# Entering the last feed-forward by token halves, and other lengths for the side work

## The chip, the cores and the metric

The kernel runs on one NeuronCore of a Trainium2 chip. The metric is the device time of one execution in microseconds (us). The engines are TensorE (PE, with its weight loads PEld), VectorE (DVE), ScalarE (ACT) and GpSimd (POOL); SyncE (SP) issues the weight DMAs. All of them run in order and wait for each other through semaphores.

## The reference

Two transformer blocks follow each other on 256 tokens of width 1024, in fp32. The first mixes softmax attention ("fox"), a gated delta rule and stick-breaking attention, then does a cross-attention to a memory and a feed-forward with a convolution. The second is this one:

```python
h = rmsnorm_2(x, ffn1_pre_g[l])
f = swiglu(h, ffn1_w_gate[l], ffn1_w_up[l], ffn1_w_down[l])
x = x + MACARON_WEIGHT * rmsnorm_2(f, ffn1_post_g[l])
h = rmsnorm_2(x, mix_pre_g[l])
proj = h @ w_in[l]
...
attn = moba_attention(to_heads(q), to_heads(k), to_heads(v), slopes)
pool = multiscale_pool(p_in, pool_w[l], pool_scale[l])
y = jnp.concatenate([attn, pool], axis=-1) @ w_out[l]
x = x + rmsnorm_2(y, mix_post_g[l])
h = rmsnorm_2(x, xa_pre_g[l])
mem_n = rmsnorm_2(mem, mem_g[l])
c = memory_cross_attention_2(h, mem_n, xa_wq[l], xa_wkv[l], xa_wo[l])
x = x + rmsnorm_2(c, xa_post_g[l])
h = rmsnorm_2(x, ffn2_pre_g[l])
f = swiglu(h, ffn2_w_gate[l], ffn2_w_up[l], ffn2_w_down[l])
x = x + MACARON_WEIGHT * rmsnorm_2(f, ffn2_post_g[l])
```

`swiglu` is `(silu(h @ w_gate) * (h @ w_up)) @ w_down` with an inner width of 2816. With 256 tokens the MoBA attention is causal attention over one block.

## The kernel before

**Chunks.** All weight matrices are cut into 178 chunks of 1 MB (`build_chunks`). SP loads chunk c into one of three buffers `raw`, once VectorE has freed it. ScalarE rounds it to fp32r (`hi`, line 1443, `whi`), VectorE takes the rest (`lo`, line 1693, `wlo`), and TensorE multiplies three products (high by high, high by low, low by high) in place of one fp32 product. `hi` and `lo` of chunk c+2 are queued when chunk c is multiplied (`LEAD`). A chunk has two halves, `("mm", c, 0)` and `("mm", c, 1)`. Kinds of chunk: W (256 output features by all 256 tokens; for each of 8 slices k of the inner axis four matmuls, of 512 and of 256 columns, lines 1139 and 1142), V and R (tokens by features, 24 matmuls of 512 columns, lines 1158 and 1170), A and O. A group of R chunks ("rows") adds up `w_out_2`, `xa_wo_2` or a down projection in four PSUM banks, two for each half of the tokens (128).

**Seams.** At the end of such a group comes the norm. For each token half: `post1` (ACT, square with sum, line 1668), `post_r` (1671, 1672), `post0` (DVE, by the gain, 1937), `post2` (DVE, into the residual `x_tok`, 1942); then for the next layer's norm `ns` (ACT, square with sum, 1461), `nr` (1465, 1466) and `nd` (DVE, times 1/rms, 1703). TensorE then transposes (`nt`, line 1184) 128x128 pieces by five groups of slices, ScalarE writes the high part of the transposed, scaled slice (`nh`, 1472), VectorE the low part (`nl`, 1708), and the next chunk's matmuls wait for `nl` of their slice. In the seam into the last feed-forward (chunks 143, 144 are the last two of `xa_wo_2`, chunk 145 is the first gate chunk) each R chunk is multiplied for both token halves, except the last one, which does token half 0 first and then token half 1.

**Side work and its planner.** Attention heads and the delta rule are chains of small steps ("links": `sc` scores, `sm` row maximum, `ex` exp, `pn` normalize, `pt` transpose, `pc` copy, `pv` values, `oc` and `ol` high and low part of the output). `build_plan` writes the order of all engines at build time. It keeps a rough clock for every engine, advanced by the costs in `ROUGH`. Between halves and quarters of chunks (`mma` is the first quarter of a half) `hook` asks `fits` for each chain whether the inputs of its next link are ready by the clock of TensorE plus a tolerance `EARLY`, and if so places that link there. Nothing is reordered on the chip, so a link put too early makes its engine wait with everything behind it. Heads of one attention run in two lanes with banks 4, 5 and 6, 7.

**Banks.** PSUM has 8 banks. `take` notes who read a bank last, and the next user waits for that step (`bank_wait`). An R chunk waits at its start for the readers of both token halves' banks.

## Time and profile before

| | us |
|---|---|
| median of 3 runs | 1211.7 |
| lowest and highest | 1209.04, 1212.9 |
| profiled execution, its own time | 1205.77 |
| its span, first to last instruction | 1204.0 |

| engine | busy us | share of the span |
|---|---|---|
| PE | 1156.5 | 96% |
| PEld | 1005.7 | 84% |
| DVE | 811.0 | 67% |
| ACT | 614.9 | 51% |
| POOL | 80.9 | 7% |

The span runs from the first to the last instruction of the core; the execution's own time has a little more around it. Busy TensorE is counted from modelled ends of matmuls, so that the gaps between its instructions are what can be read best. In a timeline each row is one or several merged instructions with start, duration, engine, line, what is written from what, and in brackets how long the engine had been idle and what released it. In a table of windows PEclk is the granted TensorE clock, 1.00 for 2.4 GHz and 0.50 for 1.2 GHz.

### The profile page before, as it was taken

Reading aid. Unit: us, or ns where it says so; the run is one execution under the profiler, and the core shown is the slowest. Engines: PE = TensorE matmul, PEld = TensorE weight load, DVE = VectorE, ACT = ScalarE, POOL = GpSimd, SP = SyncE. Lnnn points to the kernel's source line nnn. Section 1 sums busy time; section 2 is a strip of 40 time slices with the busy share of each in tenths; the row PEclk is TensorE's granted clock in tenths of the full one; section 3 lists DMA queues with packets and bytes.
Section 4 is the critical chain, followed back from the end, with each engine's and each line's share of the span. In section 5 each row is a group of like instructions: output and inputs, shape, how many; then the busy total and the mean of one; then the engine's idle time right before and its main releaser. Section 6 shows DMA issues by size and latency. Waiting matters only on the chain.

```text
span 1204.0 us, 16670 instructions
## 1 busy us (share of the span) xinstructions
PE 1156.5 (96%) x6747; PEld 1005.7 (84%) x6747; DVE 811.0 (67%) x865; ACT 614.9 (51%) x780; POOL 80.9 (7%) x114
## 2 busy tenths in 40 slices
PE   6999999999998899999999999999999997999997
PEld 6878988888987789999888888888776886888886
DVE  6877565855778667787647777647666656777743
ACT  6556344434767556555436444436345546444442
POOL 8001100200000000000000000002700000000000
PEclk9999999999999999999999999999999998999999
DMA  8644332433565336555665656555443524666550
GB/s 255 189 143 138 105 106 82 130 105 105 210 210 173 108 104 202 191 188 176 210 197 166 197 177 202 182 201 182 167 140 105 178 85 142 191 192 192 181 203 36
DMA packets 144132, 193.95 MB, mean 161 GB/s; under 512 B 6136, under 2 KB 121208, under 8 KB 144056
## 3 DMA queue, kind: packets, MB, share of 16 engines
q1 hardware_dynamic: 142856, 188.43, 48.1%
q0 software_dynamic: 1200, 4.46, 1.0%
q8 instruction: 54, 0.88, 0.3%
q14 instruction: 22, 0.18, 0.0%
HBM read 191.82 MB, written 1.05 MB: 160 GB/s over the span
## 4 chain that ended last, share of the span: by engine, by line
PE 85%; DVE 7%; ACT 4%; issue 2%; DMA 1%; SPq 0%; ACTq 0%; DVEq 0%
PE banks L1139 23%; PE banks L1170 19%; PE banks L1131 13%; PE banks L1142 11%; PE banks L1158 5%; DVE wlo L1693 2%; PE banks L1149 2%; ACT whi L1443 2%; PE banks L1383 1%; PE banks L1184 1%; PE banks L1214 1%; PE banks L1303 1%; PE banks L1257 1%; PE banks L1266 1%; DMA raw<-in_w_in 1%
## 5 line engine op out<-in xcount | busy, mean ns | idle before, releaser
L1693 DVE TENSOR_TENSOR wlo<-raw,whi 128x2048 fp32r<-128x2048 f32 x178 | 407.4, 2292 | 187.7 <-ACT whi L1443 187.6
L1443 ACT ACTIVATE whi<-raw 128x2048 fp32r<-128x2048 f32 x178 | 339.4, 1910 | 182.2 <-PE banks L1170 88.5
L1139 PE MATMUL banks<-xhl,whi 128*128 128x512 f32 x1248 | 403.9, 405 | 3.4 <-DVE fq_ L1968 1.6
L1142 PEld LDWEIGHTS banks<-xhl,wlo 128*128 128x128 f32 x1248 | 235.7, 189 | 55.8
L1142 PE MATMUL banks<-xhl,wlo 128*128 128x256 f32 x1248 | 246.9, 279 | 0.0
L1139 PEld LDWEIGHTS banks<-xhl,whi 128*128 128x128 f32 x1248 | 192.6, 190 | 11.8 <-issue 6.9
L1131 PE MATMUL banks<-xhl,whi 128*128 128x256 f32 x912 | 165.0, 284 | 0.0
L1131 PEld LDWEIGHTS banks<-xhl,whi 128*128 128x128 f32 x912 | 142.1, 192 | 0.5 <-DVE xhl L1708 0.2
L1131 PE MATMUL banks<-xhl,wlo 128*128 128x256 f32 x456 | 129.0, 283 | 0.0
L1170 PE MATMUL banks<-whi,hh 128*128 128x512 f32 x264 | 102.7, 389 | 0.0
L1170 PE MATMUL banks<-wlo,hh 128*128 128x512 f32 x264 | 102.7, 389 | 0.0
L1170 PE MATMUL banks<-whi,hl 128*128 128x512 f32 x264 | 102.7, 389 | 0.0
L1131 PEld LDWEIGHTS banks<-xhl,wlo 128*128 128x128 f32 x456 | 87.5, 192 | 0.0
L1662 ACT ACTIVATE hh<-SG 128x512 fp32r<-128x512 f32 x33 | 20.9, 632 | 93.0 <-DVE SG L1984 93.0
L1170 PEld LDWEIGHTS banks<-whi,hl 128*128 128x128 f32 x264 | 49.6, 188 | 10.4
L1170 PEld LDWEIGHTS banks<-whi,hh 128*128 128x128 f32 x264 | 49.6, 188 | 10.1
L1170 PEld LDWEIGHTS banks<-wlo,hh 128*128 128x128 f32 x264 | 49.6, 188 | 10.1
L1980 DVE TENSOR_REDUCE CA<-banks 128x512 f32<-128x1024 f32 x22 | 27.0, 1225 | 25.9 <-PE banks L1142 25.9
L1950 DVE SCALAR_TENSOR_TENSOR CA<-banks,pcol,CA 128x255 f32<-128x255 f32 (+1 forms) x88 | 36.4, 476 | 8.4 <-ACT CA L1644 8.0
L1988 DVE TENSOR_TENSOR hl<-SG,hh 128x512 fp32r<-128x512 f32 x33 | 22.9, 693 | 27.3 <-ACT hh L1662 27.3
L1158 PE MATMUL banks<-whi,xhl 128*128 128x512 f32 x96 | 35.1, 422 | 0.0
L1708 DVE SCALAR_TENSOR_TENSOR xhl<-banks,pcol,xhl 128x256 fp32r<-128x256 f32 x56 | 24.2, 479 | 8.8 <-ACT xhl L1472 8.7
(354 smaller groups left out, 1505.5 us busy)
## 6 DMA issues: line engine op xcount, KB each, us to landing
raw<-in_w_in SPq DMA_DIRECT2D x40, 1024.0 KB, 5.3
raw<-in_w_up SPq DMA_DIRECT2D x22, 1024.0 KB, 5.1
...
```

The lines of the kernel that those rows point to most:

```text
L1131: ins = pe.matmul(o, a[:, k, cols_], v[:, k, :], start=(k == 0 and i == 0), stop=(k == KD - 1 and i == 2))
L1139: pe.matmul(bank(b[m]), wh[:, k, m * P:(m + 1) * P], both[:, k, :, :].rearrange("p a t -> p (a t)"), start=(k == 0), stop=(k == KD - 1), s ...
L1142: ins = pe.matmul(bank(b[m])[:, 0:T], wl[:, k, m * P:(m + 1) * P], Xh[:, k, :], start=False, stop=(k == KD - 1), skip_group_check=True)
L1149: ins = pe.matmul(bank(b[part])[:, m * T:(m + 1) * T], a[:, k, o:o + P], v[:, k, :], start=(k == 0 and i == 0), stop=(k == NH - 1 and i == 2))
L1158: ins = pe.matmul(bank(b[t]), v[:, k, t * P:(t + 1) * P], a[:, kk, :], start=(k == 0 and i == 0), stop=(k == KD - 1 and i == 2))
L1170: ins = pe.matmul(bank(b[2 * t + nb]), v[:, k, t * P:(t + 1) * P], a[:, kk, nb * 512:(nb + 1) * 512], start=(ch["first"] and kk == 0 and i ...
L1443: act.activation(whi[c % RING][:, :], raw[c % RING][:, :], ACT.Copy).then_inc(act_done, 1)
L1693: dve.tensor_tensor(wlo[c % RING][:, :], raw[c % RING][:, :], whi[c % RING][:, :], ALU.subtract).then_inc(dve_done, 1)
L1708: dve.scalar_tensor_tensor(l_[:, k, :], turned(name, k), pcolumn(name, k), h_[:, k, :], ALU.mult, ALU.subtract).then_inc(dve_done, 1)
L1950: ins = dve.scalar_tensor_tensor(d, bank(chunks[c]["banks"][0])[:, m * T:(m + 1) * T - s], pcolumn("ffn_conv", (2 - s) * 2 * KF + a * KF + ...
L1980: dve.tensor_reduce(mat(CA[i % 2][:, 1, :]), halves(c), AX_X, ALU.add).then_inc(dve_done, 1)
L1988: dve.tensor_tensor(hl[:, 2 * i:2 * i + 2, :], mat(SG[i % 2]), hh[:, 2 * i:2 * i + 2, :], ALU.subtract).then_inc(dve_done, 1)
```

## The change

It has three parts.

1. **The seam into the last feed-forward** (`seam` in place of two `mm` and a `norm_turn`). Chunks 143 and 144 are multiplied for token half 0 first, then both for token half 1. The norm of half 0 is queued while half 1 is still multiplied. Transposes (`nt2`), high parts (`nh2`) and low parts (`nl2`) are done for each token half by itself, 128 wide and not 256, 8 and 8. The first gate chunk is multiplied by token halves too: for each slice two matmuls of 2x128 columns and two of 128, once for each half. The banks of the last feed-forward's chunks are exchanged (gate and up start in 0 to 3, the down projection adds up in 4 to 7), and `hi` and `lo` of chunk 146 come later.
2. **The pooled products one chunk sooner.** The pooling's matmuls (`pl_mm`) are placed in chunk 129 and no more in chunk 130, and in banks 0 and 1, not 2 and 3. `w_out_2` takes its banks in the order (2, 3, 0, 1), and an R chunk waits for the banks of a token half only when it comes to that half.
3. **Other lengths for the planner.** `ROUGH` has costs for each kind of attention, chunk costs go by kind, `hi` cannot end before the DMA of its chunk (5.8 us after the `lo` that frees the buffer), a link that begins on DVE or ACT is compared with that engine's clock, `EARLY` goes from 0.2 to 0.5, the turn of `mem_g_2` may not come before `add` of the chunk before, and the MoBA heads of a lane are two short chains joined.

VectorE at the seam into the last feed-forward, before (L1693 is `lo`, L1937 and L1942 `post0` and `post2`, L1703 `nd`, L1708 `nl`, L1975 the first gate chunk's reduction):

```order
L1693 TENSOR_TENSOR wlo<-raw,whi 128x2048 x3
L1937 SCALAR_TENSOR_TENSOR xs<-banks,gain 128x1024
L1942 SCALAR_TENSOR_TENSOR x_tok<-xs,small,x_tok 128x1024
L1937 SCALAR_TENSOR_TENSOR xs<-banks,gain 128x1024
L1942 SCALAR_TENSOR_TENSOR x_tok<-xs,small,x_tok 128x1024
L1703 TENSOR_SCALAR xs<-x_tok,small 128x1024 x2
L1708 SCALAR_TENSOR_TENSOR xhl<-banks,pcol,xhl 128x256 x8
L1693 TENSOR_TENSOR wlo<-raw,whi 128x2048
L1975 TENSOR_REDUCE CA<-banks 128x512
```

and after (L1793 `lo`, L2044 and L2049 `post0` and `post2`, L1803 `nd`, L1814 `nl2`):

```order
L1793 TENSOR_TENSOR wlo<-raw,whi 128x2048 x2
L2044 SCALAR_TENSOR_TENSOR xs<-banks,gain 128x1024
L2049 SCALAR_TENSOR_TENSOR x_tok<-xs,small,x_tok 128x1024
L1803 TENSOR_SCALAR xs<-x_tok,small 128x1024
L2044 SCALAR_TENSOR_TENSOR xs<-banks,gain 128x1024
L1814 SCALAR_TENSOR_TENSOR xhl<-banks,pcol,xhl 128x128 x3
L2049 SCALAR_TENSOR_TENSOR x_tok<-xs,small,x_tok 128x1024
L1814 SCALAR_TENSOR_TENSOR xhl<-banks,pcol,xhl 128x128 x5
L1803 TENSOR_SCALAR xs<-x_tok,small 128x1024
L1793 TENSOR_TENSOR wlo<-raw,whi 128x2048
L1814 SCALAR_TENSOR_TENSOR xhl<-banks,pcol,xhl 128x128 x8
L1793 TENSOR_TENSOR wlo<-raw,whi 128x2048
```

The `lo` of chunk 146 moved from ahead of `post0` to between `nd` of token half 1 and the eight `nl2` of that half.

VectorE at the first MoBA heads, before (L1863 and L1865 are `pn`, L1849 to L1857 `sm`, L1693 `lo` of chunk 130):

```order
L1863 RECIPROCAL small<-small 128x2
L1865 TENSOR_SCALAR S<-S,small 128x128
L1865 TENSOR_SCALAR S<-S,small 128x256
L1863 RECIPROCAL small<-small 128x2
L1865 TENSOR_SCALAR S<-S,small 128x128
L1865 TENSOR_SCALAR S<-S,small 128x256
L1849 SCALAR_TENSOR_TENSOR S<-cmask,banks 128x384
L1852 TENSOR_REDUCE small<-S 128x1 x2
L1857 TENSOR_SCALAR small<-small 128x2
L1693 TENSOR_TENSOR wlo<-raw,whi 128x2048
```

and after (L1970 and L1972 are `pn`, L1956 to L1964 `sm`, L1793 the `lo`):

```order
L1970 RECIPROCAL small<-small 128x2
L1972 TENSOR_SCALAR S<-S,small 128x128
L1972 TENSOR_SCALAR S<-S,small 128x256
L1970 RECIPROCAL small<-small 128x2
L1972 TENSOR_SCALAR S<-S,small 128x128
L1972 TENSOR_SCALAR S<-S,small 128x256
L1793 TENSOR_TENSOR wlo<-raw,whi 128x2048
L1956 SCALAR_TENSOR_TENSOR S<-cmask,banks 128x384
L1959 TENSOR_REDUCE small<-S 128x1 x2
L1964 TENSOR_SCALAR small<-small 128x2
```

The `lo` now stands before the `sm` of head 2. On TensorE the first quarter of chunk 128 stands ahead of the transposes of head 0 (chunk 128 came after them).

TensorE in the memory branch, before (L1158 is chunk 47, `mv`; L1184 the transposes of `mem_g_2`; L1214 the sum `hn_sum` of `mq0`):

```order
L1158 MATMUL banks<-whi,mhl 128x512 x2
L1158 MATMUL banks<-wlo,mhl 128x512
L1158 MATMUL banks<-whi,mhl 128x512
L1184 MATMUL banks<-ident,xs 128x128 x16
L1158 MATMUL banks<-whi,mhl 128x512
L1158 MATMUL banks<-wlo,mhl 128x512
L1158 MATMUL banks<-whi,mhl 128x512 x2
L1158 MATMUL banks<-wlo,mhl 128x512
L1158 MATMUL banks<-whi,mhl 128x512
L1214 MATMUL banks<-S,ones 128x512
```

and after (L1233 is chunk 47, L1307 the sum, L1262 the transposes):

```order
L1233 MATMUL banks<-whi,mhl 128x512 x2
L1233 MATMUL banks<-wlo,mhl 128x512
L1233 MATMUL banks<-whi,mhl 128x512 x2
L1233 MATMUL banks<-wlo,mhl 128x512
L1233 MATMUL banks<-whi,mhl 128x512 x2
L1233 MATMUL banks<-wlo,mhl 128x512
L1233 MATMUL banks<-whi,mhl 128x512
L1307 MATMUL banks<-S,ones 128x512
L1262 MATMUL banks<-ident,xs 128x128 x16
L1233 MATMUL banks<-whi,mhl 128x512
```

The transposes moved behind the whole of chunk 47 and behind the sum.

The core of the diff:

```diff
-EARLY, EARLY_LONG = 0.2, 0.8
+EARLY, EARLY_LONG = 0.5, 0.6
...
-         "sc": 1.3, "sm": 1.4, "ex": 0.85, "pn": 0.8, "pt": 0.7, "pc": 0.5, "pv": 0.7, "oc": 0.4, "ol": 0.45,
...
+         ("sc", "moba"): 0.65, ("sm", "moba"): 1.5, ("ex", "moba"): 0.95, ("pn", "moba"): 0.85, ("pt", "moba"): 0.67,
...
-            behind = self.ended["mm", args[0] - RING, 1]
+            behind = max(self.ended["mm", args[0] - RING, 1], self.ended["lo", args[0] - RING] + 5.8)
...
-                b = 4 * ((left + f - 1) % 2)
+                b = 4 * (left % 2)
...
-    rows("w_out_2", 4, "y5", "post", 0, (2, 3, 0, 1))
+    rows("w_out_2", 4, "y5", "post", (2, 3, 0, 1), (2, 3, 0, 1))
...
-    ffn(2, "ffn2_w_gate_2", "ffn2_w_up_2", "ffn2_w_down_2", 0, "post", 0)
+    for ch in out[-2:]:
+        ch["by_token"] = True
+    first = len(out)
+    ffn(2, "ffn2_w_gate_2", "ffn2_w_up_2", "ffn2_w_down_2", 0, "post", 4)
+    out[first]["by_token"] = True
...
+        first_ = "pe" if callable(link_[0]) else link_[0][0]
+        if first_ != "pe":
+            return ready_ <= max(pl.clock["pe"], pl.clock[first_]) + EARLY
...
+    def seam(c, name, base):
+
+        last_, gate_ = c + 1, c + 2
...
+        split(c + LEAD)
+        pl.add("pe", "mm", c, 0)
+        pl.add("pe", "mm", last_, 0)
+        pl.add("act", "post1", last_, 0)
+        pl.add("dve", "post0", last_, 0)
+        pl.add("act", "post_r", last_, 0)
+        pl.add("dve", "post2", last_, 0)
+        pl.add("pe", "mm", c, 1)
+        pl.add("act", "hi", last_ + LEAD)
+        norm_scale(name, 0)
+        pl.add("pe", "mm", last_, 1)
...
+        pl.bank_wait["nt", name, 4] = [("nl2", name, 0, turns(name)[0][-1])]
...
+        pl.add("act", "post1", last_, 1)
+        pl.add("dve", "post0", last_, 1)
+        for j in groups:
+            pl.add("pe", "nt2", name, 0, j)
+        halves_of(0, 0, 1)
+        pl.add("act", "post_r", last_, 1)
+        pl.add("dve", "post2", last_, 1)
+        halves_of(0, 2, 3, 4)
+        norm_scale(name, 1)
+        pl.add("dve", "lo", last_ + LEAD)
...
+        pl.add("pe", "mm", gate_, 0)
+        for j in groups:
+            pl.add("pe", "nt2", name, 1, j)
+        halves_of(1, *groups)
+        split(gate_ + LEAD)
+        pl.add("pe", "mm", gate_, 1)
...
-    finished[id(turn_m2)] = pl.ended["nd", "mem_g_2", 1]
+    finished[id(turn_m2)] = max(pl.ended["nd", "mem_g_2", 1], pl.ended["add", c - 1])
...
-        side.append(heads_of("moba", [lane, lane + 2, lane + 4, lane + 6]))
...
+        side.append(heads_of("moba", [lane, lane + 2]) + heads_of("moba", [lane + 4, lane + 6]))
...
-    pl.take(("pl_mm",), (2, 3), ("pl_l",))
-    mm(c, mid=[("pe", "pl_mm"), ("act", "pl_h"), ("dve", "pl_l")])
...
+    pl.take(("pl_mm",), (0, 1), ("pl_l",))
+    mm(c + 2, mid=[("pe", "pl_mm"), ("act", "pl_h"), ("dve", "pl_l")])
...
-                for t in () if 0 not in quarters else (part, 1) if ch["kind"] == "R" and part == 0 else (part,):
+                for t in () if ch["kind"] == "R" or 0 not in quarters else (part,):
...
+                elif ch["kind"] == "W" and ch["by_token"]:
+                    both, s = BOTH[ch["x"]], slice(part * P, (part + 1) * P)
+                    for k in range(KD):
+                        pe.wait_ge(dve_done, at(*plan.fresh[c], part, k))
+                        for m in range(2):
+                            pe.matmul(bank(b[m]).rearrange("p (a t) -> p a t", a=2)[:, :, s], wh[:, k, m * P:(m + 1) * P],
+                                      both[:, k, :, s], start=(k == 0), stop=(k == KD - 1), skip_group_check=True)
+                        for m in range(2):
+                            ins = pe.matmul(bank(b[m])[:, s], wl[:, k, m * P:(m + 1) * P], Xh[:, k, s], start=False,
+                                            stop=(k == KD - 1), skip_group_check=True)
...
+                        for step in plan.bank_wait.get(("mm", c, half), []) if part == 0 else []:
+                            pe.wait_ge(DONE[plan.engine[step[0]]], at(*step))
```

## Rows read from the trace of the kernel before

**Rows 1.** The page: busy us and share; line engine | busy, mean ns.

```profile
...
PE 1156.5 (96%) x6747; PEld 1005.7 (84%) x6747; DVE 811.0 (67%) x865; ACT 614.9 (51%) x780; POOL 80.9 (7%) x114
...
L1443 ACT ACTIVATE whi<-raw 128x2048 fp32r<-128x2048 f32 x178 | 339.4, 1910 | 182.2 <-PE banks L1170 88.5
```

**Rows 2.** Waits of TensorE: releaser, us, times, longest us.

```profile
...
PE banks L1184 <- DVE xs L1703: 7.0, 2, 6.8
...
PE banks L1184 <- DVE mq_ L1968: 2.7, 1, 2.7
...
PE banks L1170 <- DVE qk_ L1968: 2.2, 1, 2.2
```

**Rows 3.** Timeline of TensorE, memory branch.

```profile
...
385.13 2.72 PE L1184 MATMUL banks<-ident,xs 128*128 128x128 f32 x16 [2.71 <-DVE mq_ L1968]
```

**Rows 4.** Windows: busy PE, PEld, DVE, ACT, POOL; granted clock, DMA.

```profile
...
386.00:390.00 4.00, 4.00 (x17) 3.54 (x16) 4.00 (x9) 3.20 (x8) 0.00 (x0) 0.57 0.67 235
867.00:871.00 4.00, 4.00 (x14) 2.81 (x13) 1.34 (x4) 2.17 (x5) 0.00 (x0) 0.57 0.00 0
1007.00:1014.00 7.00, 2.73 (x13) 2.73 (x14) 3.73 (x6) 4.12 (x12) 0.64 (x2) 0.52 0.35 127
1014.00:1015.00 1.00, 1.00 (x8) 0.91 (x7) 1.00 (x3) 0.97 (x3) 0.00 (x0) 0.91 0.00 0
```

**Rows 5.** Timeline of TensorE at the first MoBA heads.

```profile
...
862.66 0.39 PE L1158 MATMUL banks<-wlo,xhl 128*128 128x512 f32 x1
862.89 0.39 PE L1158 MATMUL banks<-whi,xhl 128*128 128x512 f32 x1
865.85 0.55 PE L1361 MATMUL banks<-ident,S 128*128 128x128 f32 x3 [2.57 <-DVE S L1865]
```

**Rows 6.** Waits of TensorE in the MoBA stretch.

```profile
...
PE banks L1170 <- DVE y5l L1878: 1.2, 1, 1.2
PE banks L1361 <- DVE y5l L1878: 1.1, 2, 0.7
```

**Rows 7.** Timeline of TensorE, end of the cross-attention.

```profile
...
974.21 0.95 PE L1363 MATMUL banks<-ident,S 128*128 128x128 f32 x7 [1.63 <-DVE y5l L1878]
```

**Rows 8.** Timeline of the seam into the last feed-forward.

```profile
...
1001.10 2.29 DVE L1693 TENSOR_TENSOR wlo<-raw,whi 128x2048 fp32r<-128x2048 f32 x1 [3.15 <-ACT whi L1443]
...
1001.86 1.03 ACT L1668 ACTIVATE xs<-banks 128x1024 f32<-128x1024 f32 x1 [0.79 <-PE banks L1170]
...
1003.42 1.22 DVE L1937 SCALAR_TENSOR_TENSOR xs<-banks,gain 128x1024 f32<-128x1024 f32 x1
...
1004.10 0.39 PE L1170 MATMUL banks<-whi,y5l 128*128 128x512 f32 x1
...
1004.68 1.28 DVE L1942 SCALAR_TENSOR_TENSOR x_tok<-xs,small,x_tok 128x1024 f32<-128x1024 f32 x1
...
1008.64 1.06 ACT L1461 ACTIVATE xs<-x_tok 128x1024 f32<-128x1024 f32 x1 [0.65 <-DVE x_tok L1942]
...
1010.46 0.75 DVE L1703 TENSOR_SCALAR xs<-x_tok,small 128x1024 f32<-128x1024 f32 x1 [1.12 <-ACT small L1466]
...
1011.27 3.36 PE L1184 MATMUL banks<-ident,xs 128*128 128x128 f32 x16 [6.78 <-DVE xs L1703]
...
1013.77 3.01 DVE L1708 SCALAR_TENSOR_TENSOR xhl<-banks,pcol,xhl 128x256 fp32r<-128x256 f32 x7 [0.73 <-ACT xhl L1472]
...
1020.34 1.22 DVE L1975 TENSOR_REDUCE CA<-banks 128x512 f32<-128x1024 f32 x1 [0.22 <-PE banks L1142]
```

**Rows 9.** Groups of VectorE, 92 to 290 us.

```profile
...
L1834 DVE SCALAR_TENSOR_TENSOR gS<-gS,gX,banks 128x128 f32<-128x128 f32 x16 | 4.5, 344 | 7.5 <-PE banks L1305 7.5
```

**Rows 10.** Groups of ScalarE, 92 to 290 us.

```profile
...
L1547 ACT ACTIVATE gKt<-banks,gcols 128x128 f32<-128x128 f32 x8 | 3.1, 386 | 0.0
```

**Rows 11.** Timeline of TensorE: transposes in a stream.

```profile
...
938.96 1.69 PE L1184 MATMUL banks<-ident,xs 128*128 128x128 f32 x14
```

**Rows 12.** Waits of TensorE, fox and delta rule.

```profile
...
PE banks L1257 <- DVE gY L1813: 0.7, 3, 0.4
```

81 lines of the change are left out of this document (61 added, 20 removed), and 7 rows, old and new, of the table ROUGH.

## Prediction, made before the changed kernel ran

> **What bounds the kernel now.** I read the page first: TensorE is busy for 1156.5 us of a span of 1204.0 [rows 1]. So only what TensorE waits for, what it does at half clock, and what it does more or less of can move the time. The second view is the table of TensorE's waits. It shows one long wait, 6.8 us at the seam into the last feed-forward (`nd`, line 1703), and then 2.7, 2.6 and 2.2 us at three places in the side work [rows 2, 5]. The third is the granted clock in windows: it lay at 1.2 GHz (0.50) for a while behind three of these waits. Over 386 to 390 us its mean was 0.57, over 867 to 871 also 0.57, and over 1007 to 1014 it was 0.52 [rows 4]. In the first two stretches TensorE was busy throughout, so they cost 4.0 x (1 - 0.57) = 1.7 us each. In the third it mostly waited. The last view is the timeline of each place.
>
> **The seam, in the times of the trace before.** `post1` of token half 0 starts at 1001.86, the last matmul ends at 1004.10 + 0.39 = 1004.5, the last `nd` starts at 1010.46, the transposes at 1011.27, and the gate chunk's reduction at 1020.34 [rows 8]. Doing half 0 of chunk 144 one half earlier lets `post1` start 2.7 us earlier (half a chunk; 1004.5 less 1001.86), at 999.1. From there:
> - `post1` takes 1.1 with its accumulator read, `post0` 1.22, `post2` 1.28 [rows 8]. The `lo` that held `post0` before (1001.10 to 1003.39) is gone from there. `post2` of half 0 ends at 1002.9.
> - ScalarE has `hi` of chunk 146 queued ahead of `ns`. It waits for chunk 143 to end (1001.8) and takes 1.9 us (line 1443 [rows 1]), so `ns` starts at 1003.8. From `ns` to `nd` takes 1.8 us (1008.64 to 1010.46) and `nd` 0.75 [rows 8]: first transpose at 1006.4. The long wait shrinks from 6.8 to 1.9 us.
> - ScalarE does `post1` of half 1 from 1005.5 to 1006.65, then `nh2`. VectorE does `post0` until 1007.9, three `nl2`, `post2` until 1010.3, and the other five `nl2`. An operation of that shape (scalar_tensor_tensor, 128x128 out of PSUM) cost 4.5 / 16 = 0.28 us in a stream [rows 9], and 128x128 on ScalarE 0.39 [rows 10]. The last `nl2` of half 0 ends at 1011.8, and the token-0 half of the gate chunk with it, at 1012.3. In between TensorE waits in pieces.
> - `ns`, `nr`, `nd` of half 1 start when `post2` ends: `nd` ends at 1012.9. Now VectorE has the 2.29 us `lo` of chunk 146 [rows 8] in front of the eight `nl2` of half 1. They start at 1015.2 and end at 1017.7. Nothing needs this `lo` before the next chunk, but the `nl2` are queued behind it and TensorE behind them. TensorE has the eight transposes and can begin the token-1 half at 1015.7.
> - The token-1 half is 8 slices of four matmuls. Fourteen 128-column transposes, each with its own weights, took 1.69 us, 0.11 each after taking off the end of the last [rows 11]. I take 0.11 for the 128-column and 0.12 for the 256-column ones: 0.45 a slice, 3.6 us, end at 1019.4. Bound below: columns alone, half of the (1020.2 - 1014.6) = 5.6 us of the chunk before, 2.8 us. Bound above: all at 1.2 GHz, at least twice 2.8.
>
> Before, the chunk ended at about 1020. So the seam as a whole gives 0.5 us, although its wait falls by 4.9: the rest is given back as 1.7 us more TensorE work (7.2 for 5.6) and as new waits for `nl2`. Bounds: +2.0 (columns alone, and the `nh2` without delay) and -2.0 (the clock stays low into the token-1 half). The 8 + 8 operations on ScalarE and VectorE in place of 8 have no other user waiting there. `lo` of 147 comes at 1018 to 1020.5 and is wanted at 1025. The DMA freed by `lo` of 146 lands long before its use.
>
> The Trainium skill, TensorE: Matmul & The Clock Gate, section "LDWEIGHTS", says a weight load takes its number of columns over 1.2 GHz, whatever streams. That speaks against this part: 64 loads of 128 columns for the gate chunk would be an estimated 6.8 us, not 3.4. Its section "Back-to-back issue gap" has about 81 ns for a pair at 128 columns, by which a half would be an estimated 2.6 us. By the first the seam gives the 0.5 us, by the second an estimated 1.5. The transposes at 0.11 [rows 11] agree with the first.
>
> **The memory branch.** The transposes of `mem_g_2` waited 2.71 us for an `add` on `mq_`, after only a quarter of chunk 47 had been issued [rows 3]. Now the remaining 18 matmuls of that chunk (about 4.1 us) and a sum stand in front of them. They need nothing late, and the `add` has then ended. The wait goes, and with it the cause of the slow stretch of [rows 4]: 2.7 + 1.7 = 4.4 us. Bounds: 2.7 if the clock falls anyway, 5.0 with small gaps behind it.
>
> **The MoBA stretch.** The transposes of head 0 waited 2.57 us for `pn` [rows 5]. Now the first quarter of chunk 128 is ahead of them: six matmuls at 0.23 (862.66 to 862.89 [rows 5]), 1.4 us. The wait is 1.2, and I expect the clock to stay up: 1.4 + 1.7 [rows 4]. `lo` of chunk 130 is now ahead of `sm` of head 2 and delays that head by 2.3 us, but its transposes come two chunks later. The wait of 2.2 us for `add` on `qk_` [rows 2] was `w_out_2` asking for banks 0 and 1, which chunk 130 had just written. Now half 0 goes to banks 2 and 3, read long ago, and a score step and half 1 come later: 2.2 gone. The pooled products come at about 876 in their new place and I cost them at nothing: their windows on GpSimd are done before that, and the banks' reader is the copy of chunk 128, which ends then; were it late, they would wait as they did before, some tenths. Of the waits for `y5l`, the last, 1.2 us before chunk 134, stays. The two of 1.1 together become one of about 0.7 (its longest [rows 6]), since copy, values and output of head 7 follow one another with nothing beside them: 0.4. Sum 5.7 us. Bounds: 3.5 (clock still low, another 0.5 in waits) and 7.
>
> **The cross-attention's end.** `pv` of head 0 is now ahead of the last half of chunk 140, so `y5l` comes earlier. Its wait of 1.63 us [rows 7] becomes 0.3, and `sc` of head 3 gets a wait of 0.3 for the `add` now behind `pn` and `ol`: 1.0 (0.5 to 1.5).
>
> **Fox and delta rule.** Some 36 pieces on TensorE stand elsewhere. The wait that recurs there before is 0.7 us in 3 [rows 12], so nothing is to be won, and the tolerance of 0.5 allows small new waits. I cost it at 0.5 us; bounds +0.5 and -1.5.
>
> **Sum.** 0.5 + 4.4 + 5.7 + 1.0 - 0.5 = 11.1 us less. The profiled execution took 1205.77 (span 1204.0 and 1.8 around it), so a like one would take 1194.7. The median of the runs shown is 1211.7, 5.9 above the profiled one, and the forecast for a median is 1200.6.
>
> **Rivals.**
> - *The clock does not come back.* The low stretches follow the new waits (1.2 us at head 0, the pieces at the seam). For: the clock fell behind waits of 2.6 and 2.7 us, so little is missing. Against: a wait of 1.2 is less than half of either. Then 3.4 us less is won: 1204.
> - *The seam is dearer.* TensorE runs in short pieces from 1006 to 1015, the clock stays at 1.2 GHz as in 1007 to 1014 [rows 4], and the token-1 half takes 7.2 in place of 3.6: 1204.2. Against: the clock was back at 0.91 in 1014 to 1015 [rows 4] after 3 us of transposes only.
> - *The seam is cheaper.* Narrow matmuls go by their columns and waits fall further: 1.5 to 2 us more, 1198.8.
> - *The change does not do what it says in the side work.* VectorE's queue only moves the MoBA waits: only the 2.2 there, the memory branch, and nothing else, 6.1 us: 1205.6.
> - *Slower.* Links put early by the larger tolerance make TensorE wait at piece after piece in fox and delta rule, where it is busy without pause. It decides from 11.6 / 36 = 0.32 us a piece. The longest there before is 0.4 [rows 12]. At 0.4 each it is 14.4 us, the total 1211.7 - 11.6 + 14.4 = 1214.5. Against: VectorE has room there and the new costs are closer to the trace.
>
> **How the numbers follow.** Forecast 0.50 (its own range 1198 to 1203), clock 0.19, seam dearer 0.08, seam cheaper 0.10, side work 0.08, slower 0.05. About 0.3% (3.6 us) is what a measurement can tell from no change here, since the three runs before lie 3.9 us apart. The bounds add up to savings between 3.2 and 16; two medians scatter by 2 us. I leave out a tenth at each end: 1195 to 1207. Faster (under 1208.1) 0.88: all cases but the last, less 0.07 for two of them together. Within 0.3% 0.07, slower 0.05.
>
> **What would show it.** No wait before the transposes of `mem_g_2`, clock 1.00 over that place and over the first MoBA heads, a wait of about 1.2 us at head 0, none before chunk 131. At the seam: first transposes 1.9 us after the last row matmul, `nl2` of half 1 in one stream right behind a `lo`, and 14.9 us (before 15.5) from the last row matmul to the end of the gate chunk. A saving at the seam of several us, or a `nl2` stream that starts with `nd`, would make that step wrong. Waits of 0.3 us and more by the dozen between 90 and 290 us would make the whole wrong.

## The result and the profile after

| | before | after |
|---|---|---|
| median of 5 runs, side by side | 1209.38 us (1205.07 to 1212.9) | 1196.2 us (1195.82 to 1200.65) |
| profiled execution, and its span | 1205.77, 1204.0 us | 1200.3, 1198.6 us |
| mean granted clock in it | 0.991 | 0.992 |

The ratio is 0.9903, 95% interval [0.9876, 0.9931]: 11.7 us less, between 8 and 15. It is close to the ratio of the means, 1197.8 to 1209.6. The forecast was 1200.6 in 1195 to 1207. The profiled execution after is one of the two slower ones of its five, and the one before (1205.77) is near the fastest, so the two traces differ by only 5.4 us of span. They are therefore compared stretch by stretch. The length of a stretch is taken between two matmuls that both kernels have.

| stretch | before | after | difference | forecast |
|---|---|---|---|---|
| start to the 400th matmul | 69.5 | 71.6 | +2.1 | 0 |
| to the first matmul on the memory tokens (fox, delta rule) | 284.8 | 285.9 | +1.0 | +0.5 |
| to the first matmul on the memory branch's output | 67.2 | 63.5 | -3.6 | -4.4 |
| to the first down-projection | 148.3 | 149.9 | +1.6 | 0 |
| to the cross-attention's first value chunk (MoBA) | 358.3 | 352.4 | -6.0 | -5.7 |
| to the last row matmul | 76.0 | 75.0 | -1.0 | -1.0 |
| to the end (the seam) | 199.5 | 199.9 | +0.3 | -0.5 |

The page's line on the engines (busy us; share of the span; instructions) against [rows 1]:

```profile
PE 1161.4 (97%) x6779; PEld 1011.5 (84%) x6779; DVE 811.4 (68%) x873; ACT 616.5 (51%) x788; POOL 82.2 (7%) x114
```

There are 32 matmuls more (the gate chunk by halves) and eight operations more on each of VectorE and ScalarE, as the diff says. TensorE is busy for 4.9 us longer in a span that is 5.4 us shorter: its idle time fell from 47.5 to 37.2 us.

TensorE's waits (releaser; us, times, longest us) against [rows 2, 6, 12]:

```profile
PE banks L1277 <- DVE xs L1803: 2.0, 1, 2.0
...
PE banks L1277 <- DVE xhl L1814: 1.3, 2, 1.0
PE banks L1350 <- DVE gY L1920: 1.3, 5, 0.5
PE banks L1454 <- DVE S L1972: 1.2, 1, 1.2
PE banks L1248 <- DVE y5l L1985: 1.2, 1, 1.2
...
PE banks L1430 <- DVE mq_ L1880: 0.8, 1, 0.8
...
PE banks L1307 <- DVE mq_ L1880: 0.5, 1, 0.5
...
PE banks L1456 <- DVE y5l L1985: 0.2, 1, 0.2
```

The 6.8 at the seam is 2.0 and 1.3. The 2.7 on `mq_` and the 2.2 on `qk_` are gone, with 0.8 and 0.5 new in the memory branch. The 2.6 at MoBA's head 0 is 1.2. The 1.63 at the end of the cross-attention is 0.2. `gY` in the delta rule takes 1.3 in five where it took 0.7 in three.

Windows of the changed kernel (us; busy PE, PEld, DVE, ACT, POOL; granted clock; DMA share, GB/s), against [rows 4]:

```profile
390.00:394.00 4.00, 4.00 (x27) 3.37 (x26) 2.46 (x6) 2.85 (x7) 0.00 (x0) 1.00 0.76 231
...
422.00:426.00 4.00, 4.00 (x14) 3.21 (x13) 2.29 (x1) 1.11 (x3) 0.00 (x0) 0.57 0.08 20
...
866.00:870.00 4.00, 2.97 (x15) 2.17 (x16) 3.01 (x7) 3.23 (x6) 1.48 (x2) 1.00 0.11 44
...
1002.00:1009.00 7.00, 6.42 (x30) 6.45 (x31) 6.33 (x12) 3.83 (x12) 0.64 (x2) 0.52 0.23 76
1009.00:1010.00 1.00, 1.00 (x10) 1.00 (x10) 0.15 (x1) 0.21 (x1) 0.00 (x0) 0.92 0.00 0
```

The clock is up behind `mem_g_2` and at the MoBA heads, where it was 0.57 before. At 422 us there is a stretch at 1.2 GHz that the trace before did not have: that is the +1.6 of the table. At the seam TensorE is now at 1.2 GHz while it works (6.42 of 7 us busy). Before, it was at 1.2 GHz mostly while it waited (2.73 of 7).

The timeline of the seam (start, us, engine, line, operation, [idle before]), against [rows 8]:

```profile
998.28 0.39 PE L1248 MATMUL banks<-whi,y5l 128*128 128x512 f32 x1
1000.62 0.98 PE L1277 MATMUL banks<-ident,xs 128*128 128x128 f32 x7 [1.95 <-DVE xs L1803]
1002.58 0.45 PE L1277 MATMUL banks<-ident,xs 128*128 128x128 f32 x1 [0.97 <-DVE xhl L1814]
1002.71 0.76 PE L1203 MATMUL banks<-xhl,whi 128*128 128x256 f32 x2
...
1003.59 0.73 PE L1203 MATMUL banks<-xhl,whi 128*128 128x256 f32 x2
...
1009.39 0.96 PE L1277 MATMUL banks<-ident,xs 128*128 128x128 f32 x7
...
1012.23 0.45 PE L1203 MATMUL banks<-xhl,whi 128*128 128x256 f32 x2
...
1012.69 0.45 PE L1203 MATMUL banks<-xhl,whi 128*128 128x256 f32 x2
...
1014.53 0.67 PE L1214 MATMUL banks<-xhl,whi 128*128 128x512 f32 x2
```

The first wait is 1.95 us. The token-0 half runs without a pause, at 0.85 us a slice (1002.71 to 1003.59 and on), since the clock is low. Only behind it come the transposes of half 1 (1009.39). The token-1 half takes 0.46 a slice (1012.23 to 1012.69) and ends at 1014.5, 15.86 us after the last row matmul. Before, it was 15.57.

On VectorE in the same place:

```profile
1006.20 0.75 DVE L1803 TENSOR_SCALAR xs<-x_tok,small 128x1024 f32<-128x1024 f32 x1 [0.63 <-ACT small L1559]
1006.86 2.28 DVE L1793 TENSOR_TENSOR wlo<-raw,whi 128x2048 fp32r<-128x2048 f32 x1
1010.19 0.35 DVE L1814 SCALAR_TENSOR_TENSOR xhl<-banks,pcol,xhl 128x128 fp32r<-128x128 f32 x1 [1.04 <-ACT xhl L1572]
1010.85 2.18 DVE L1814 SCALAR_TENSOR_TENSOR xhl<-banks,pcol,xhl 128x128 fp32r<-128x128 f32 x7 [0.31 <-ACT xhl L1572]
```

The `lo` does stand between `nd` and the `nl2` of half 1. But VectorE waits 1.04 us behind it for ScalarE, which waits for the transposes: in this execution the `lo` holds nothing up.

The first MoBA heads, against [rows 5]:

```profile
867.03 0.55 PE L1454 MATMUL banks<-ident,S 128*128 128x128 f32 x3 [1.20 <-DVE S L1972]
```

The end of the cross-attention, against [rows 7]: the wait for `y5l` at head 0 and the new one for `qk_` at the scores of head 3.

```profile
968.01 1.06 PE L1456 MATMUL banks<-ident,S 128*128 128x128 f32 x8 [0.24 <-DVE y5l L1985]
969.27 1.96 PE L1436 MATMUL banks<-xk_,qk_ 128*128 128x256 f32 x8 [0.20 <-DVE qk_ L2075]
```

### The profile page after: what moved, and what is told of

Read it like the earlier page. It is cut to its first block, busy times and chain, and to the rows that moved or that the text cites. A ratio compares the mean times of both kernels' runs of the same rounds, so it can differ in the third digit from the quotient of the medians.

```text
span 1198.6 us, 16754 instructions
## 1 busy us (share of the span) xinstructions
PE 1161.4 (97%) x6779; PEld 1011.5 (84%) x6779; DVE 811.4 (68%) x873; ACT 616.5 (51%) x788; POOL 82.2 (7%) x114
## 4 chain that ended last, share of the span: by engine, by line
PE 87%; DVE 6%; ACT 4%; issue 2%; DMA 1%; SPq 0%; ACTq 0%; DVEq 0%
PE banks L1214 24%; PE banks L1248 20%; PE banks L1196 14%; PE banks L1217 12%; PE banks L1233 4%; PE banks L1224 2%; DVE wlo L1793 2%; ACT whi L1536 2%; PE banks L1476 1%; PE banks L1307 1%; PE banks L1350 1%; PE banks L1396 1%; PE banks L1359 1%; DMA raw<-in_w_in 1%; PE banks L1436 1%
## 5 line engine op out<-in xcount | busy, mean ns | idle before, releaser
L1793 DVE TENSOR_TENSOR wlo<-raw,whi 128x2048 fp32r<-128x2048 f32 x178 | 407.4, 2293 | 180.8 <-ACT whi L1536 180.7
L1214 PE MATMUL banks<-xhl,whi 128*128 128x512 f32 x1232 | 399.1, 405 | 3.4 <-DVE fq_ L2075 1.6
L1214 PEld LDWEIGHTS banks<-xhl,whi 128*128 128x128 f32 x1232 | 190.1, 190 | 12.0 <-issue 6.8
L1233 PE MATMUL banks<-whi,xhl 128*128 128x512 f32 x96 | 34.9, 418 | 0.0
L1102 POOL TENSOR_TENSOR gMs<-gM,lev 128x512 f32<-128x512 f32 x12 | 21.3, 1776 | 139.0 <-DVE gM L1901 96.6
```

The costliest lines, as they stand in the source:

```text
L1102: pool.tensor_tensor(gMs[l % 2][:, :, :], gM[:, :, :], lev[:, l, :].unsqueeze(1).to_broadcast([P, NH, P]), ALU.mult).then_inc(pool_done, 1)
L1214: pe.matmul(bank(b[m]), wh[:, k, m * P:(m + 1) * P], both[:, k, :, :].rearrange("p a t -> p (a t)"), start=(k == 0), stop=(k == KD - 1), s ...
L1233: ins = pe.matmul(bank(b[t]), v[:, k, t * P:(t + 1) * P], a[:, kk, :], start=(k == 0 and i == 0), stop=(k == KD - 1 and i == 2))
L1793: dve.tensor_tensor(wlo[c % RING][:, :], raw[c % RING][:, :], whi[c % RING][:, :], ALU.subtract).then_inc(dve_done, 1)
```

## Experiments

All of them are read by the stretches of the same table. Where a run took one execution only, its total says little and its trace is what counts. Short stretches at 1.2 GHz (low stretches below) come at different places in different executions; each costs 1.7 us where TensorE is busy (3.4 us long: 4 us at a mean of 0.57 in [rows 4]). So the places are given with each time.

### The seam taken back, and the seam alone

`no_seam` is the changed kernel with the seam of before:

```diff
...
-    seam(c + 2, "ffn2_pre_g_2", 4)
-    pl.add("pool", "gain_load", 3)
-    c += 5
-    for _ in range(KF + KF // 2 - 1):
+    mm(c + 2)
+    mm(c + 3)
+    c += 4
+    pl.add("pool", "gain_load", 3)
+    norm_turn("ffn2_pre_g_2", 0)
+    for _ in range(KF + KF // 2):
...
```

> The changed kernel with the old seam into the last feed-forward (whole chunks, whole turns, old banks there); parts 2 and 3 stay. Theory 1 (the seam gives nothing, since what it wins in waiting it pays in narrow matmuls and low clock): 11 to 12 us under before, within 1 us of the changed kernel; from the last row matmul to the end of the gate chunk 15.5 us as before, against 15.9 in the changed kernel. Theory 2 (the seam is where the gain is): only 5 to 8 us under before.

Measured: 1198.76 us (1194.75 to 1200.18, 6 runs), 0.9892 [0.987, 0.9914] of before. The changed kernel has 0.9903 [0.9876, 0.9931]. That is 13 us less than its own runs of before, where the first theory said 11 to 12: the gain is there without the seam.

`seam_only` is the kernel before with part 1 alone: costs, tolerances, banks, pooled products and MoBA chains stay as in before (the lines are against the changed kernel).

```diff
...
-EARLY, EARLY_LONG = 0.5, 0.6
+EARLY, EARLY_LONG = 0.2, 0.8
...
-    rows("w_out_2", 4, "y5", "post", (2, 3, 0, 1), (2, 3, 0, 1))
+    rows("w_out_2", 4, "y5", "post", 0, (2, 3, 0, 1))
...
```

> The kernel before with part 1 alone (seam by token halves and the exchanged banks of the last feed-forward). Theory 1: within 1 us of before, TensorE's wait before the first transposes down from 6.8 to about 1.9 us, the gate chunk's end 15 to 16 us behind the last row matmul as before. Theory 2: 3 to 5 us faster than before.

Measured: 1209.11 us (1205.74 to 1213.12, 12 runs), 0.9989 [0.9975, 1.0004] of before: 1.3 us less, between 3.0 less and 0.5 more. In its trace the gate chunk ends 15.73 us after the last row matmul, and in that of `no_seam` 15.49. What follows from both: the seam is worth between nothing and 3 us of the 11.7.

### The gate chunk whole

`gate_whole` keeps the rows and the norm by halves, but takes the gate chunk in one piece behind both (`halves_of(1, ...)` first, then `mm(gate_, 0)` and `mm(gate_, 1)`).

```diff
-    out[first]["by_token"] = True
...
-        pl.add("pe", "mm", gate_, 0)
         for j in groups:
             pl.add("pe", "nt2", name, 1, j)
...
+        pl.add("pe", "mm", gate_, 0)
         pl.add("pe", "mm", gate_, 1)
```

> The changed kernel, but the first gate chunk is multiplied whole (512 and 256 columns) after both token halves are turned. If the narrow matmuls are the price (7 us of TensorE for 5.6), the stretch from the last row matmul to the end of the gate chunk gets shorter than 15.9 us, about 15. If the token-0 half is in the shadow of the waits for nd of half 1 anyway, it gets longer: nl2 of half 1 starts 10.5 us behind the last row matmul, the first slice follows, and 5.6 us of gate chunk end at 16.5 us or later.

Measured: 1198.69 us in one run; the gate chunk ends 19.1 us after the last row matmul, and from there to the end of the kernel it is 203.1 us, against 15.9 and 199.9. It gets longer, as the second branch of the expectation said, and by more than its 16.5. TensorE (timeline of this kernel):

```profile
1002.17 1.76 PE L1276 MATMUL banks<-ident,xs 128*128 128x128 f32 x7 [3.98 <-DVE xs L1802]
...
1004.85 1.19 PE L1213 MATMUL banks<-xhl,whi 128*128 128x512 f32 x2
...
1006.27 1.05 PE L1213 MATMUL banks<-xhl,whi 128*128 128x512 f32 x2
```

Without the token-0 half TensorE waits 3.98 us for the `nd` of half 1, and the clock stays low for 13.7 us. Halving the chunk therefore buys 3.2 us (one trace of each, and one seam differs by up to 1.4 between traces, see below), and the halved rows and norm without it are worse than the seam of before. The seam stands or falls by the gate chunk.

### The clock held up in the seam

`warm_seam` is the changed kernel with eight idle matmuls of 512 columns in the 1.95 us wait; `warm_lo_late` has them too, and `lo` of chunk 146 behind the `nl2` of half 1.

```diff
+        pl.add("pe", "warm")
         for j in groups:
             pl.add("pe", "nt2", name, 0, j)
...
+            def warm():
+                ...
+                for i in range(8):
+                    ins = pe.matmul(bank(7), y5h[:, i % 4, 0:P], ..., start=True, stop=True)
```
```diff
-        pl.add("dve", "lo", last_ + LEAD)
...
         halves_of(1, *groups)
+        pl.add("dve", "lo", last_ + LEAD)
```

> The changed kernel with eight extra matmuls of 512 columns (1.8 us, their result is overwritten) on TensorE between the last row matmul and the first transposes, where it waits 1.95 us. Theory 1 (the low clock from 3.7 to 10.5 us behind the last row matmul is what holds the token-0 half until 10.7 us): the clock stays at 2.4 GHz or falls later, the token-0 half ends with nl2 at about 7.5 us, and the gate chunk ends at 14.5 us in place of 15.9; the nl2 of half 1 still wait for lo of chunk 146. Theory 2 (the clock follows the pieces of work behind, not this wait): the clock falls at the same place and the stretch stays at 15.9 us.

> The changed kernel with eight idle 512-column matmuls in the wait after the last row matmul, and with the lo of chunk 146 put behind the nl2 of token half 1 on VectorE. Theory (two causes add up: the low clock costs the seam about 0.9 us, and the lo in front of the nl2 of half 1 costs whatever part of its 2.3 us lies on the path when the clock is up): the gate chunk ends 13 to 13.5 us after the last row matmul, 198 us or less from there to the end. Rival (the lo is hidden in this form too, because the token-0 half of the gate chunk is what ends last there): 15.0 and 199.0 again, as with the idle matmuls alone.

`warm_seam` measured 1199.06 us in one run; the gate chunk ended 15.0 us after the last row matmul and the kernel 199.0 us after it: 0.9 us less than the changed kernel. A low stretch came all the same, later and half as long, and the token-0 half ended at 9.8 us where the theory had 7.5:

```profile
1000.00:1004.00 4.00, 2.82 (x21) 2.35 (x20) 3.58 (x7) 3.60 (x12) 0.00 (x0) 1.00 0.00 2
1004.00:1008.00 4.00, 3.78 (x19) 3.79 (x20) 3.36 (x7) 1.65 (x4) 0.64 (x2) 0.57 0.35 131
1008.00:1010.00 2.00, 1.66 (x16) 1.45 (x14) 1.54 (x4) 1.40 (x5) 0.00 (x0) 1.00 0.07 12
```

`warm_lo_late` measured 1196.86 us in one run, 199.8 from the last row matmul to the end. The first `nl2` of half 1 starts 10.64 us after the last row matmul in both (1008.94 in `warm_seam` and 1005.95 here):

```profile
1002.84 0.75 DVE L1812 TENSOR_SCALAR xs<-x_tok,small 128x1024 f32<-128x1024 f32 x1 [0.63 <-ACT small L1568]
1005.95 0.35 DVE L1823 SCALAR_TENSOR_TENSOR xhl<-banks,pcol,xhl 128x128 fp32r<-128x128 f32 x1 [2.36 <-ACT xhl L1581]
```

VectorE now idles 2.36 us where the `lo` was, so the `lo` was free, and moved it is late: the next chunk waits 0.57 us for it. For this form the theory that it costs part of its 2.3 us is wrong, and the rival right: in both kernels the token-0 half ended last, at 9.8 us.

That does not hold for every execution of the new seam. In the trace of `start_warm` (its own edit is at the start, see below) the low stretch ended 5.6 us after the last row matmul, and the token-0 half was done at 8.5:

```profile
1004.86 2.28 DVE L1798 TENSOR_TENSOR wlo<-raw,whi 128x2048 fp32r<-128x2048 f32 x1
...
1007.07 2.15 DVE L1819 SCALAR_TENSOR_TENSOR xhl<-banks,pcol,xhl 128x128 fp32r<-128x128 f32 x8
...
1007.56 0.30 PE L1282 MATMUL banks<-ident,xs 128*128 128x128 f32 x1 [1.48 <-DVE xhl L1819]
```

ScalarE began the high parts of half 1 at 1005.52. In the changed kernel the `nl2` followed that by 0.40 us (1009.79 to 1010.19); here they follow by 1.55, in one stream right behind the `lo`, and TensorE's last transpose waits 1.48 us for them. So when the clock is up early the `lo` costs an estimated 1.2 us (1.55 less 0.40), as the prediction had it. No run has an early rise and the `lo` moved.

`old_seam_fill` is `no_seam` with 28 such matmuls in the 6.8 us wait (the same kind of edit, ahead of `norm_turn`).

> The changed kernel with the seam of before, and 28 idle 512-column matmuls in the 6.8 us in which TensorE waited there. Theory (the clock falls because TensorE idles, and half clock costs that seam 3.4 us of work at half speed, some of it behind VectorE's nl anyway): the granted clock stays at 1.00 through the seam, the gate chunk ends 13.8 to 14.5 us after the last row matmul, against 15.5, and about 198 us from there to the end. Rival (the nl on VectorE, not TensorE, set the end of the gate chunk): the clock stays up and the chunk still ends at 15.3 or later.

Measured: 1198.44 us in one run. Windows of it:

```profile
998.00:1005.00 7.00, 6.82 (x31) 5.30 (x29) 5.73 (x6) 4.92 (x12) 0.64 (x2) 1.00 0.55 179
1005.00:1008.00 3.00, 2.75 (x21) 2.54 (x22) 1.52 (x4) 2.16 (x5) 0.00 (x0) 1.00 0.28 109
```

The clock stays at 2.4 GHz. The gate chunk ends at 14.27, and the kernel 198.2 us after the last row matmul, the shortest together with `best_filled` below: the seam of before with a filled wait beats the new seam of the changed kernel, at half clock, by 1.7 us. Put side by side, the end of the gate chunk (taken at the next chunk's first matmul) after the last row matmul in each trace, with the length of the low stretch there:

| seam of before | | new seam | |
|---|---|---|---|
| before | 15.57 (6.8) | after | 15.86 (6.8) |
| no_seam | 15.49 (6.8) | seam_only | 15.73 (6.8) |
| mem_alone | 15.82 (6.8) | start_warm | 14.70 (3.4) |
| mem_fill_free | 16.07 (6.8) | warm_seam, with filler | 15.0 (3.4) |
| moba_alone | 16.34 (6.8) | | |
| mem_fill | 16.86 (10.2) | warm_lo_late, with filler | 15.73 (3.4), 0.57 of it the wait for `lo` |
| old_seam_fill, best_filled | 14.27 (0) | | |

The three of the new seam without filler average 15.43, the six of the old one 16.03: 0.6 us for the new. That spread over executions is as wide as what was to be decided, so one pair of traces could not have told it.

### The memory branch: the wait, and the clock behind it

`mem_fill` and `mem_fill_free` are the kernel before with 22 idle transposes ahead of those of `mem_g_2`, into bank 0, and then into bank 5 (the lines are the second one's):

```diff
+                if (name, j) == ("mem_g_2", 0):
+                    pe.wait_ge(dve_done, at("nl", "norm_xq", KD - 1))
+                    for i in range(22):
+                        pe.transpose(bank(5)[:, 0:P], ident[:, :], ident[:, :])
                 pe.wait_ge(dve_done, at("nd", name, 1))
```

> The kernel before with 22 idle transposes of 128 columns in the wait of 2.7 us ahead of the transposes of mem_g_2; nothing else is changed, so what the kernel waited for still takes as long. Theory (the slow stretch of 3.4 us behind that place comes from the wait): no slow stretch begins near 386 us, and the way from the first matmul of the memory branch to its last one before w_mem_out is 1.6 to 1.8 us shorter than before (67.2 us before, 65.5 then). Rival A (the stretch is not caused by the wait): it comes at 385 to 387 us all the same, 67.2. Rival B (transposes do not keep the clock up): as A, although TensorE is not idle.

> The kernel before with 22 idle transposes of 128 columns in the wait of 2.7 us ahead of the transposes of mem_g_2, this time into bank 5, which nothing holds then (in the first form they went to bank 0 and stood behind the wait themselves). Theory (the slow stretch behind that place comes from TensorE's idling): the wait is 0.1 us, no slow stretch begins between 384 and 392 us, and the way from the first matmul on the memory tokens to the first on the branch's output is 65.4 to 65.6 us, against 67.2 before. Rival A (the stretch has another cause): it comes all the same, 67.2. Rival B (transposes do not hold the clock up): as A; then with rival A excluded by the runs in which the wait is gone and the stretch with it.

`mem_fill` (1216.65 us in one run) missed its aim: bank 0 is what TensorE waited for, so the transposes stood behind the 2.67 us and not in it. A low stretch began at 388.2 all the same, and the memory stretch was 69.7 us.

```profile
387.78 4.29 PE L1183 MATMUL banks<-ident 128*128 128x128 f32 x22 [2.67 <-DVE mq_ L1973]
```

`mem_fill_free` (1210.72 us in one run) put them in the wait:

```profile
384.92 2.56 PE L1182 MATMUL banks<-ident 128*128 128x128 f32 x22
387.81 1.94 PE L1188 MATMUL banks<-ident,xs 128*128 128x128 f32 x16 [0.33 <-DVE mq_ L1972]
```
```profile
384.00:388.00 4.00, 3.67 (x29) 3.25 (x28) 3.93 (x4) 3.10 (x4) 0.00 (x0) 1.00 0.33 82
388.00:392.00 4.00, 4.00 (x25) 3.26 (x24) 4.00 (x7) 3.36 (x8) 0.00 (x0) 1.00 0.76 245
```

No low stretch follows, and the memory stretch of the table takes 65.6 us against 67.2. So the wait itself cost 2.7 and the clock behind it 1.6. All four traces with this wait unfilled have a low stretch behind it (385.6 to 388.2 us), and this one has none: transposes hold the clock too, as far as one trace shows it. A low stretch then came at 422 us, as in the changed kernel.

`mem_alone` is the kernel before with the two edits for this place:

```diff
-    finished[id(turn_m2)] = pl.ended["nd", "mem_g_2", 1]
+    finished[id(turn_m2)] = max(pl.ended["nd", "mem_g_2", 1], pl.ended["add", c - 1])
...
-            behind = self.ended["nd", "norm_mem", 1] + 9.0
+            behind = self.ended["nd", "norm_mem", 1] + 11.0
```

> The kernel before with the change's two edits for the memory branch alone (the norm turn of mem_g_2 is held until the sum of the chunk before has ended in the plan; its ns comes 2 us later in the plan). TensorE's order there becomes that of the changed kernel. Theory: no wait and no slow stretch near 386 us, 62.8 us from the first matmul on the memory tokens to the first on the branch's output (67.2 less 2.7 less 1.7), up to 63.6 with the two small waits of 0.5 and 0.8 that the changed kernel shows. Rival (the gain in the changed kernel needs its new costs too): the wait moves to another place there, 65 or more.

Measured: 1210.06 us in one run, 63.7 us for the memory stretch. The two edits give the whole 3.5 us, with no wait at the transposes and a new one of 0.51 us behind them (and 0.76 later):

```profile
391.82 1.02 PE L1214 MATMUL banks<-S,ones 128*128 128x512 f32 x2
392.68 1.91 PE L1184 MATMUL banks<-ident,xs 128*128 128x128 f32 x16
...
399.21 1.10 PE L1214 MATMUL banks<-S,ones 128*128 128x512 f32 x2 [0.51 <-DVE mq_ L1773]
```

Its total is that of before: against the trace before its start took 2.2 us longer, and the two stretches with the low ones at 196, 275, 285 and 425 us took 5.2 longer.

### The MoBA part without the planner's costs

`moba_alone` is the kernel before with `w_out_2` in banks 2, 3, 0, 1, the pooled products one chunk sooner in banks 0 and 1, the waits by halves and the chains of two.

```diff
...
-    rows("w_out_2", 4, "y5", "post", 0, (2, 3, 0, 1))
+    rows("w_out_2", 4, "y5", "post", (2, 3, 0, 1), (2, 3, 0, 1))
...
-    pl.take(("pl_mm",), (2, 3), ("pl_l",))
+    pl.take(("pl_mm",), (0, 1), ("pl_l",))
```

> The kernel before with part 2 of the change alone (w_out_2 in banks 2, 3, 0, 1 with a wait for each half, the pooled products one chunk sooner in banks 0 and 1, heads 4 to 7 of MoBA as chains of two); costs and tolerances as before, so the transposes of head 0 stand where they stood. Theory: the wait of 2.6 us at head 0 and the slow stretch behind it stay, the waits of 2.2 and 0.3 for sums on qk_ go and 0.4 of those for y5l: the way from the first matmul of w_out_2 to the cross-attention's first value chunk is 34.0 to 35.3 us against 35.6, and the stretch from the last feed-forward matmul to w_out_2 is 2.0 to 2.6 us shorter. Rival (the planner's costs carry the MoBA gain): less than 1 us of both together.

Measured: 1206.9 us in one run; the MoBA stretch is 356.2 us against 358.3 before and 352.4 after. Waits of TensorE over its whole span:

```profile
PE banks L1363 <- DVE S L1867: 4.2, 3, 2.6
```

The 2.2 for `qk_` is gone, the 2.6 at head 0 is still there, and two new ones (0.74 and 0.85) stand at the next heads' transposes. So banks and chains give 2.2 of the 6.0 us. By difference the other 3.8 come from the new costs and tolerances, which put a quarter of chunk 128 ahead of head 0 (1.4 of wait, and the clock) and the later heads where they wait less; no run has these alone, and which cost or tolerance does it is not shown. Of the two parts that were expected, the one up to `w_out_2` was 1.0 us and not 2.0 to 2.6, and the one behind it 1.2, within the 0.3 to 1.6.

### The start, and everything together

`start_warm` is the changed kernel with idle fp32 matmuls of 128 columns before the parameters arrive (10) and before the first transposes (6).

```diff
+                for i in range(10):
+                    pe.matmul(bank(7)[:, 0:P], ident[:, :], ident[:, :], start=True, stop=True)
                 pe.wait_ge(par_in, 16)
```

> The changed kernel with idle fp32 matmuls of 128 columns at the very start: ten before the parameters arrive (about 2 to 6.5 us) and six before the first transposes (7.5 to 10.3 us), where TensorE waited for DMA and VectorE. Theory (the granted clock rises only some time after TensorE begins to work, 14 to 19 us into the kernel so far): it rises before the first real matmuls at 14.3 us, and the first chunk of projections runs at 0.22 us a matmul of 256 columns from the start; 2 to 3 us less than the profile of the changed kernel up to its 400th matmul. Rival (the rise is tied to time since the start and not to the work): it rises at 13 to 19 us as before, and the time is the same.

Measured: 1197.11 us in one run. The first transposes of the changed kernel, and then those and the first projections here:

```profile
10.29 3.25 PE L1262 MATMUL banks<-ident,gates 128*128 128x128 f32 x14 [2.82 <-DVE gates L1803]
```
```profile
10.48 1.75 PE L1267 MATMUL banks<-ident,gates 128*128 128x128 f32 x14 [1.88 <-DVE gates L1808]
14.58 0.41 PE L1267 MATMUL banks<-ident,gates 128*128 128x128 f32 x2 [2.35 <-DVE xhl L1813]
...
15.54 0.40 PE L1198 MATMUL banks<-xhl,whi 128*128 128x256 f32 x2
...
15.94 0.63 PE L1198 MATMUL banks<-xhl,whi 128*128 128x256 f32 x2
```

Fourteen transposes take 1.75 us where they took 3.25, so the clock was up by then. But the time saved turned into a wait of 2.35 us for `nl`, and behind that wait the clock fell (0.63 a pair from 15.94). Right in its mechanism, nothing in time. (A 256-column matmul at full clock takes 0.12 us here, 0.36 for the three of a slice, and not the 0.22 of the expectation.)

`best_filled` is `old_seam_fill` with the start filled through (10, 11 and 8 matmuls, the last 8 in that 2.35 us) and four more before the gate rows at 56 us.

> The changed kernel with the seam of before, and idle matmuls wherever TensorE waited long enough: 28 of 512 columns in the 6.8 us of the seam, and fp32 ones of 128 columns at the start (ten from 2 us on, eleven from 7.1, eight from 12.2 us, where the clock fell back after a wait of 2.35 us in the run with fewer of them, four before the gate rows at 56 us). Theory (the clock is held up by work of any kind, and only the clock was lost there): the clock is up from 5 to 6 us on without falling back before 50 us, 2.0 to 2.5 us less up to the 400th matmul of the projections; the seam without a slow stretch, 198.2 us from the last row matmul to the end against 199.9; 1.7 more if the stretch at 59 us goes. Together 1192 to 1195 us, about 0.3% less than the changed kernel. Rival A (the early rise is paid back later, or the idle matmuls delay a load or a step): within 1 us of the changed kernel, 1195 to 1198. Rival B (idle matmuls queue in front of real ones): slower than it.

Measured: 1195.07 us (1192.38 to 1195.09, 5 runs), 0.9872 [0.985, 0.9894] of before. The changed kernel has 0.9903 [0.9876, 0.9931], measured at another time against other runs of before, so 1.1 us between the medians and overlapping intervals don't show it faster, though all five runs lie below the changed kernel's fastest. The start and the stretch at 59 us in its trace:

```profile
10.51 1.75 PE L1277 MATMUL banks<-ident,gates 128*128 128x128 f32 x14 [0.57 <-DVE gates L1820]
...
15.92 0.40 PE L1198 MATMUL banks<-xhl,whi 128*128 128x256 f32 x2
```
```profile
55.00:63.00 8.00, 7.97 (x44) 5.71 (x42) 5.45 (x7) 3.16 (x5) 0.00 (x0) 1.00 0.66 211
```

At the start the durations tell the clock (0.40 us for the pair that took 0.63 in `start_warm`). The granted clock in the windows does not: up to its first change it reads 1.00 in the changed kernel too, whose transposes run at half speed there. The low clock at the start, at 59 us and at the seam is gone, and a place near 75 us is reached 3.1 us sooner than in `no_seam`. This execution had low stretches at 181 and 280 us, which took 3.4 of it back.

## Why the prediction came out as it did

- **The whole.** The forecast was 4.4 us too high. Its base was 2.3 us too high: the three runs shown had a median of 1211.7, and the five side by side, these three among them, have 1209.38. The saving was 0.6 too low: the ratio says 11.7 us where 11.1 were forecast. The other 1.5 are the medians: the five runs after are two near 1200.5 and three near 1196, and their median lies 1.6 below their mean. That 11.7 meets 11.1 is in part luck. The terms of the table that belong to the change (all but the start and the 422 us) sum to 9.3. The interval of 8 to 15 holds that, so the other 2.4 need no cause of their own. One that would fit is low stretches at places that vary. Outside the start, 59, 386 and 867 us, the seam and the end, the six traces with the order of before on at least one of the two removed waits hold 15 lengths of 3.4 us, 2.5 each, and the eight with all of part 3 hold 9, 1.1 each; the difference at 1.7 us is about 2.3. Three of the fifteen are between 894 and 900 us, at the 2.2 us wait for `qk_` [rows 2], in three of the five kernels that have this wait, and there is none in the nine that don't. The prediction took that wait at its own length only. That the count is more than chance isn't shown.
- **The seam.** Right: the wait (1.9 forecast, 1.95), the narrow slices (0.45, 0.46), `lo` between `nd` and `nl2`, starting 8.4 us after the last row matmul (8.2). Wrong: the step that ended the token-0 half at 7.8 us, with VectorE as its limit; it ended at 10.7. TensorE was at 1.2 GHz and 0.85 us a slice, which made it the limit. The prediction looked for the low clock in the token-1 half and named that as a rival, but the clock had come back by then (0.92 in 1009 to 1010); it was the half before that paid. With it the step on `lo` failed in this trace: it stands there and costs nothing, since the transposes of half 1 are late by as much. In `start_warm`, where the low stretch ended early, both steps come near to what was forecast: the token-0 half ends at 8.5 (7.8 forecast), the `nl2` stream starts right behind the `lo` at 10.4 (10.7 forecast), and the chunk ends at 14.7 (14.9 forecast). The size of the term was -0.5; one pair of traces says +0.3, three against six -0.6, the timing of the seam alone -1.3 [-3.0, +0.5].
- **The memory branch.** Right in both parts, shown apart by `mem_fill_free`: 2.7 of wait, 1.6 of clock (1.7 forecast). Mis-sized by 0.8: two waits of 0.5 and 0.8 for sums on `mq_` follow, now that TensorE no longer stops before them, and one of 0.5 for `S` went. In 3 of the 10 traces without the wait a low stretch came at 422 to 425 us, at waits of 1.1 and 1.7 us for `y2l` (in `mem_alone` one of 2.6), and in none of the three that had the stretch at 386 and no filler. Whether one follows from the other stays open.
- **MoBA.** Forecast 5.7, measured 6.0, and the parts as forecast: the wait 1.2 at head 0, the clock up, nothing before chunk 131, one wait of 0.63 near the end (0.7 forecast), the last `y5l` 1.15. What the banks and what the new costs are worth (2.2 and 3.8) the prediction had not told apart.
- **Cross-attention's end.** 1.0 forecast and measured. The 1.63 us wait [rows 7] is 0.24, and the new one at the scores of head 3 is 0.20, where 0.3 each were forecast. By these waits 1.2 us would be saved, so 0.2 stay open. No experiment takes this part by itself.
- **Fox and delta rule.** +0.5 forecast, +1.0 measured with one low stretch on each side. Longer waits for `gY` account for 0.6. The rival by which waits come by the dozen did not happen.
- **The Trainium skill** (TensorE: Matmul & The Clock Gate). By "LDWEIGHTS" the token-1 half was to be an estimated 3.4 us and by "Back-to-back issue gap" 2.6. It took 3.8 (1010.74 to 1014.53), 0.46 a slice of four: the trace agrees with the first. A rule that was not weighed: Part 4, "PE-mode transpose", has it that transposes don't engage the full clock. Here 22 of them held it up by themselves for 2.6 us in the one trace of `mem_fill_free`, so the measurement decides against it for this form (`pe.transpose` of fp32, 128x128).
